# 192 instead of 160 tokens add their experts' V rows by gather; the dense V product runs over 352 token columns

## What is computed

```
q = (x @ w_query)                               # 8 heads, 2 halves of 128
s = einsum('thpc,hpnc->thpn', q, sub_keys)      # scores against 2 x 128 keys
ids, gates = top-16 of the 16 x 16 sums per head, softmax   # 128 experts per token
h = gelu(einsum('td,thkd->thk', x, u_table[ids]))
out = einsum('thk,thkd->td', gates * h, v_table[ids])       # v_table: 16384 x 2048
x = LayerNorm(alpha * x + out)
```

## Time and profile before

| | us |
|---|---|
| median of 3 runs | 3607.54 |
| lowest, highest | 3605.48, 3608.09 |
| profiled execution, its own time | 3631.05 |
| its span, first to last instruction | 3629.3 |

### The profile page before, as it was taken

The page is one execution under the profiler, slowest core; times in us unless marked ns, Lnnn a source line. Parts: engine busy times, 40 slices in busy tenths (PEclk is TensorE's granted clock), DMA queues, the critical chain, the costliest instruction groups (busy, mean ns, idle before and its releaser), DMA issues. The chain is left out here.

```text
span 3629.3 us, 62687 instructions
## 1 busy us (share of the span) xinstructions
PE 3519.3 (97%) x25376; PEld 3466.7 (96%) x25376; DVE 2730.9 (75%) x3476; ACT 1186.3 (33%) x1155; POOL 1843.4 (51%) x1107
## 2 busy tenths in 40 slices
PE   8999999898999999999999999998899999999997
PEld 7999999898999999999999999998899999999996
DVE  4866959624899777777777777774588888888876
ACT  2332332314222234444444444443222222222223
POOL 3443533445444577868787860003366666665321
PEclk9999999899999999999999999999899999999998
DMA  4222212563235578888888887776699899999962
GB/s 152 74 75 78 80 72 79 212 254 128 82 104 177 184 211 220 224 230 219 231 224 226 224 226 229 217 229 246 236 354 357 346 356 360 347 358 351 357 264 96
DMA packets 466252, 788.24 MB, mean 217 GB/s; under 512 B 78976, under 2 KB 376384, under 8 KB 402384
## 3 DMA queue, kind: packets, MB, share of 16 engines
q1 hardware_dynamic: 337920, 547.99, 45.8%
...
## 5 line engine op out<-in xcount | busy, mean ns | idle before, releaser
L616 POOL TENSOR_TENSOR wl<-wraw,wh 128x512 fp32r<-128x512 f32 x352 | 536.3, 1554 | 696.9 <-ACT wh L1114 689.0
L667 POOL DMA_INDIRECT g_scratch<-picks,g_col x384 | 684.1, 1782 | 175.6 <-issue 148.7
L1114 ACT ACTIVATE wh<-wraw 128x2048 fp32r<-128x2048 f32 x216 | 414.0, 1917 | 1008.3 <-PE ps L1030 715.2
L1030 PE MATMUL ps<-Wh,wh 128*128 128x384 f32 x2048 | 688.4, 336 | 13.6 <-issue 6.0
L1030 PE MATMUL ps<-Wl,wh 128*128 128x384 f32 x2048 | 687.4, 336 | 6.3 <-issue 6.3
L1030 PE MATMUL ps<-Wh,wl 128*128 128x384 f32 x2048 | 687.3, 336 | 6.2 <-issue 6.1
L998 PE MATMUL ps<-xh,wl 128*128 128x272 f32 x1792 | 518.5, 289 | 0.0
L998 PE MATMUL ps<-xl,wh 128*128 128x272 f32 x1792 | 515.5, 288 | 0.0
L998 PE MATMUL ps<-xh,wh 128*128 128x272 f32 x1792 | 515.0, 287 | 0.0
L715 PE MATMUL ps<-xh,wh 128*128 128x272 f32 x2304 | 488.8, 294 | 22.2 <-DVE ext L1664 11.9
L715 PE MATMUL ps<-xh,wl 128*128 128x272 f32 x2304 | 479.4, 290 | 0.0
...
## 6 DMA issues: line engine op xcount, KB each, us to landing
wraw<-in_u_t SPq DMA_DIRECT2D x128, 1024.0 KB
...
wraw<-in_v_t SPq DMA_DIRECT2D x128, 1024.0 KB
...
```

Source lines behind the costliest of these rows:

```text
L616: ins = nc.gpsimd.tensor_tensor(wl[:, u, part], wraw[:, u, part], f(wh[:, u, part]), ALU.subtract)
L667: nc.gpsimd.indirect_dma_start(g_elem, bass.IndirectOffsetOnAxis(ap=idx, axis=0), gate, None, compute_op=ALU.add).then_inc(g_put, 16)
L1030: ins = mat(out, w[:, u, d * EG + e], m[:, e], start=(begin and e == 0 and w is wh and m is Wh[v]), stop=(end and e == EG - 1 and w is wl))
L1114: go(wh[:, u], wraw[:, u], ACT.Copy).then_inc(whi, 1)
```

## The change

TD becomes T - P - RT = 352 with RT = 64, and so SD = 192. REST is now 64 tokens, spread over NB = 2 partitions each: XSLOTS = 64, ALL = 192 slots over the same 110 steps. The dense products, `gt`, `hg`, `wt` and the additions have 352 columns. `Wh` and `Wl` keep rows of 384 (and so their places in memory). Of the third tile of 128 dense tokens, gates of only 96 are scattered; the number of scatters stays. `y_x` now gives 16 x 64 columns, twice what the bank TURN has free at once, so `fold` is done in halves: 8 matmuls of 64 columns after PE's tile m = 6 of group 14 and 8 after m = 7, with a DVE addition after each. The REST lists are packed by 6 small DMAs instead of 12.

```diff
-TD = 384
+RT, NB = 64, 2
+TD = T - P - RT
 SD = T - TD
-NGC = TD // GC
+NGC = -(-TD // GC)
-NB = P // TS
-XSLOTS = SLOTS // NB
+XSLOTS = -(-SLOTS // NB)
...
-TOPK_TILES = ((0, P), (P, P), (2 * P, P), (T - P, P), (TD, TS))
+TOPK_TILES = ((0, P), (P, P), (2 * P, P), (T - P, P), (TD, RT))
...
-        Wh = [at(f"Wh{v}", [P, EG, TD], F32R, X0 + v * 2 * EG * ROWD) for v in range(2)]
+        WROW = 384 * 4
+        Wh = [at(f"Wh{v}", [P, EG, 384], F32R, X0 + v * 2 * EG * WROW)[:, :, 0:TD] for v in range(2)]
...
-                    nc.gpsimd.dma_start(dst[to], src[:, fr]).then_inc(pk_s, 16)
+                    nc.gpsimd.dma_start(dst[to, 0:fr.stop - fr.start], src[:, fr]).then_inc(pk_s, 16)
...
-                if m == EG - 2:
-                    pe.wait_ge(y_sp_u, 4)
+                if m >= EG - 2:
+                    half = m - (EG - 2)
+                    pe.wait_ge(y_sp_u, 4 + half)
                     pe.wait_ge(y_sp_s, 2)
-                    for k in range(KT):
-                        ins = mat(ps[:, TURN, k * TS:(k + 1) * TS], y_x[:, k * P:(k + 1) * P], fold[:],
+                    for j in range(HK):
+                        k = half * HK + j
+                        ins = mat(ps[:, TURN, j * RT:(j + 1) * RT], y_x[:, k * P:(k + 1) * P], fold[:],
                                   start=True, stop=True)
                     ins.then_inc(y_turn, 1)
...
+            for x in (x_ids, x_hid, x_gate):
+                C.done(nc.vector.memset(x[:], 0), dve)
+            C.done(tt_(fold[:], ident[:, 0:RT], ident[:, RT:2 * RT], ALU.add), ids_s)
...
+                if n == (NG - 2) * EG + EG - 1:
+                    v_.wait_ge(y_turn, 5)
+                    a_ = acc[:, 0:HK, TD:T - P]
+                    C.inc(stt_(a_, a_, ALPHA, ps[:, TURN, 0:HK * RT].rearrange("p (k t) -> p k t", k=HK),
+                               ALU.mult, ALU.add), y_sp_u)
...
-            v_.wait_ge(y_turn, 5)
+            v_.wait_ge(y_turn, 6)
```

More of the change, by code:

```diff
@@ L265, in program @@
[L265 to L271 removed]
+        XB = XSLOTS * 4
+        x_ids, x_hid = [at(n, [P, XSLOTS], U32, S0 + 15520 + k * XB) for k, n in enumerate(("x_ids", "x_hid"))]
@@ new lines, in program @@
+        x_gate, x_h, x_w = [at(n, [P, XSLOTS], F32, S0 + 15520 + (2 + k) * XB) for k, n in enumerate(("x_gate", "x_h", "x_w"))]
+        fold = at("fold", [P, RT], F32, S0 + 15520 + 5 * XB)
+        o = 15520 + 5 * XB + RT * 4
+        r_ids, r_hid = [at(n, [RT, SLOTS], U32, S0 + o + k * SLOTS * 4) for k, n in enumerate(("r_ids", "r_hid"))]
+        r_f = at("r_f", [RT, SLOTS], F32, S0 + o + 2 * SLOTS * 4)
+        o += 3 * SLOTS * 4
+        assert o + 5 * SLOTS * 4 + 4 <= 21760
+        zeros = at("zeros", [P, 4, TD], F32, S0)
@@ L275, in program @@
-        Wl = [at(f"Wl{v}", [P, EG, TD], F32R, X0 + v * 2 * EG * ROWD + EG * ROWD) for v in range(2)]
-        G0 = X0 + 4 * EG * ROWD
+        WROW = 384 * 4
+        Wh = [at(f"Wh{v}", [P, EG, 384], F32R, X0 + v * 2 * EG * WROW)[:, :, 0:TD] for v in range(2)]
+        Wl = [at(f"Wl{v}", [P, EG, 384], F32R, X0 + (v * 2 + 1) * EG * WROW)[:, :, 0:TD] for v in range(2)]
+        G0 = X0 + 4 * EG * WROW
         gath = [at(f"gath{v}", [P, D], F32, G0 + v * D * 4) for v in range(3)]
@@ L361, in program @@
             sem("slots_done"), sem("slots_turned"), sem("turned_used"))
-        sh_in = [sem(f"slot_h_in{b}") for b in range(ALL // HB)]
+        sh_in = [sem(f"slot_h_in{b}") for b in range(-(-ALL // HB))]
         sv_in = [sem(f"slot_v_in{b}") for b in range(3)]
@@ L1350, in score_evict @@
                 go(sc[:, slot, 0:4].rearrange("p q k -> p (q k)"), ps[:, 4 + 2 * (slot % 2), :], ACT.Copy)
-                go(sc[0:TS, slot, 4], ps[0:TS, 5 + 2 * (slot % 2), 0:P], ACT.Copy).then_inc(s_out, 1)
+                go(sc[0:RT, slot, 4], ps[0:RT, 5 + 2 * (slot % 2), 0:P], ACT.Copy).then_inc(s_out, 1)
             for n in range(SC):
@@ L1870, in _ @@
             C.done(ts_(s_h[:], s_w[:], float(SD), s_tok[:], ALU.mult, ALU.add), dve)
-            C.done(ts_(s_h[:], s_h[:], float(TS), None, ALU.add), dve)
+            C.done(ts_(s_h[:], s_h[:], float(RT), None, ALU.add), dve)
             C.done(cp(s_hid[:], s_h[:]), dve)
             def rest(a):
-                return picks[0:TS, a, REST].rearrange("p h k -> p (h k)")
+                return picks[0:RT, a, REST].rearrange("p h k -> p (h k)")
             C.done(stt_(r_f[:], rest(1), float(P), rest(2), ALU.mult, ALU.add), dve)
             cp(r_ids[:], r_f[:])
-            C.done(ts_(r_f[:], r_f[:], float(SD), s_tok[0:TS], ALU.mult, ALU.add), dve)
+            C.done(ts_(r_f[:], r_f[:], float(SD), s_tok[0:RT], ALU.mult, ALU.add), dve)
             C.done(cp(r_hid[:], r_f[:]), dve)
-            C.done(tt_(fold[:], ident[:, 0:TS], ident[:, TS:2 * TS], ALU.add), dve)
-            for b in range(2, NB):
-                ins = tt_(fold[:], fold[:], ident[:, b * TS:(b + 1) * TS], ALU.add)
-                C.done(ins, ids_s if b == NB - 1 else dve)
+            for x in (x_ids, x_hid, x_gate):
+                C.done(nc.vector.memset(x[:], 0), dve)
+            C.done(tt_(fold[:], ident[:, 0:RT], ident[:, RT:2 * RT], ALU.add), ids_s)
             def flat(a):
@@ L2026, in slot @@
                 if s % HB == 0:
[L2027 removed]
+                    n = min(HB, ALL - s)
+                    v_.wait_ge(sh_in[s // HB], 16 * n)
                     if s < SLOTS:
@@ L2031, in slot @@
                     else:
-                        C.done(tt_(x_w[:], x_h[:], x_gate[:], ALU.mult), dve)
+                        b = slice(s - SLOTS, s - SLOTS + n)
+                        C.done(tt_(x_w[:, b], x_h[:, b], x_gate[:, b], ALU.mult), dve)
                 v_.wait_ge(sv_in[s % 3], 16 * (s // 3 + 1))
@@ L2098, in _ @@
                     slot(s)
-            v_.wait_ge(y_turn, 5)
-            a_ = acc[:, :, TD:T - P]
-            C.done(stt_(a_, a_, ALPHA, ps[:, TURN].rearrange("p (k t) -> p k t", k=KT), ALU.mult, ALU.add), dve)
+            v_.wait_ge(y_turn, 6)
+            a_ = acc[:, HK:KT, TD:T - P]
+            C.done(stt_(a_, a_, ALPHA, ps[:, TURN, 0:HK * RT].rearrange("p (k t) -> p k t", k=HK),
+                        ALU.mult, ALU.add), dve)
             nc.vector.memset(fsum1[:], 0.0)
```

31 lines of the change are left out of this document (11 added, 20 removed).

## The result

| | us |
|---|---|
| before, median of 4 runs (lowest, highest) | 3607.07 (3605.48, 3608.09) |
| after, median of 4 runs (lowest, highest) | 3622.36 (3617.20, 3627.01) |
| after / before, 95% interval | 1.0045 (1.0033 to 1.0057) |
| profiled execution of after, its span | 3617.2, 3615.4 |

The change makes the kernel 15 us slower, where 3602.5 was forecast as the likeliest time. A second measurement, at the end of the study, gave 3622.92 beside 3607.89, ratio 1.0040 (1.0018 to 1.0063).

A forecast was written before the change was run, and what follows sets the result against it. PE bound the kernel, with DVE and the transfers close behind. Groups with slots +1.9, steps without slots -9.6 and the sparse part's end +2.7 gave -5.0 us on the median 3607.54: 3602.5 us, range 3574 to 3640.

The forecast's parts named there:

- the transfers set the pace, 380 GB/s: 3623: Rival for the slot-carrying groups: coupled DMA queues hold only 380 GB/s, 68.2 us a group, 3623 us; chance 0.28 (380 to 365).
- PE's ledger, 7.68 us a step: V stage: 32 fewer columns save PE 0.64 us a step, giving 7.68 us a step, 61.4 a group of eight.
- DVE's ledger, 63.9 us a group: V stage: DVE's work rises from 59.6 to 63.9 us a group, through more slots and slightly shorter narrow operations.
- The DMA ceiling, 403 GB/s: V stage: the DMA engines can carry 403 GB/s, so a group's 25.9 MB take 64.3 us.
- How the three add up: Groups with slots: PE, DVE and DMA together give 66.7 us a group, +0.14, or +1.9 us over 13.75 groups.
- a group is 65.3 us: Groups with slots: PE's pace with DVE's uneven heavy steps, before transfers, gives 65.3 us, 1.3 less than before.
- DVE's two long tiles (8.4 and 10.6 us): V stage: DVE falls 1 us behind at m = 5 and 2.3 at m = 6, stretching two tiles to 8.4 and 10.6 us.
- POOL's ledger: V stage: a V gather and its h gather cost 4.1 us against a slot every 4.7 us, so POOL fits at 88%.
- The sentence in brackets below that ledger: POOL shares its SBUF interface with DVE; if POOL instructions lengthen as DVE fills up, that adds to the slower case.
- The steps without slots, -9.6: The 18 steps without slots, in groups 0, 14 and 15: PE gets its 0.64 us in 15, -9.6 us.
- the end, +2.7: End of the sparse part: fold of twice the columns +1.2 us, longer wait for DVE's last slot +1.5; bounds 0 and +6.
- The signs to look for: V stage: PE waits for `wl`, ACT for `wraw`, DVE for `gath`; if the last two carry the loss, transfers are the cause.

The follow-up runs named there:

- e3: The changed kernel, but each V gather fetches half of each row and DVE adds that half twice: 3603.71 us, ratio 0.9999 to the kernel before.
- e4: The changed kernel with all gathers kept, but DVE adds only half of each gathered row per slot: 3539.57 us, ratio 0.9814 to the kernel before.
- e1: The changed kernel with only 160 of its 192 slots, so narrow columns alone: 3551.08 us, ratio 0.9845 to the kernel before.
- e14: e3 with the preparation of the next group's weights spread over the group's steps: 3579.50 us, ratio 0.9897 to the kernel before.
- e5: The changed kernel with idle matmuls filling PE's waits before tiles m = 7 and m = 0 in groups 2 to 13: 3615.41 us, ratio 1.0031.
- e10: e3 with idle matmuls filling PE's waits before tiles m = 7 and m = 0: 3599.46 us, ratio 0.9967 to the kernel before.

## Why the prediction was wrong

It said 3602.5, with the bounds 3574 and 3640; 3622.4 is on the other side of no change. The time lies next to the rival "the transfers set the pace, 380 GB/s: 3623". That is a coincidence; the mechanism is not that rival's: with half the bytes (e3) groups are still 67.8 us, and with less DVE work the same bytes go at 410 GB/s (e4).

- *PE's ledger, 7.68 us a step*: right; group 15 has 7.74 and 7.73, and e1 gained 54 us.
- *DVE's ledger, 63.9 us a group*: right. The late group of after, 68.4 us, less DVE's 4.3 us of waits is 64.1, and e14 runs at 64.3.
- *The DMA ceiling, 403 GB/s*: right, if low by 2% (410 over 200 us).
  The 358 GB/s that the prediction weighed, of the Trainium skill, "DMA: Bandwidth & Descriptors", Bandwidth, is passed by 15% in e4; the measurement decides. What the page says of single-core runs, nearer to 435, agrees.
- *"How the three add up", a group of 66.7 us, +0.14*: this is the step that failed. Measured 68.9, +1.8 on a group of before, times 13 is 23.4 us in place of 1.9. (The base was low as well: the group of before, taken as 66.56, is 67.1 on average, as four of the 13 have a step of some 9.5 us.) In the prediction's own terms, "a group is 65.3 us" for DVE and PE alone was 67.8 (e3), 2.5 too low, and the transfers' 1.4 on top of it were 1.1. Three things were mis-sized:
  - *"DVE's two long tiles (8.4 and 10.6 us)"*, which are PE's tiles m = 7 and 0 with the wait before them, were 9.62 and 12.12. The lengths of DVE's heavy steps were right: 9.82, 9.65 and 10.46 from split to split for 9.7, 9.7 and 10.6. What failed is how far DVE is behind when they begin. The sum gives m = 3 one slot and so enters them ahead. By `slots_at` this holds for groups 1 to 7 only; from group 8 on the steps with one slot are m = 2 and 6, and m = 3, 4 and 5 all carry two. In e3, where hardly a transfer is late, tile m = 7 takes 8.8 to 9.4 us in groups 1 to 7 and 9.6 from group 8 on, and the eight tiles from there 67.1 and 68.3 us on average. So the shift can account for at most 1.2 us of the later groups; the earlier ones too are 1.8 above 65.3. PE waits 4.5 us for `wl` in the late group, and in the light steps behind DVE cannot make up for it, since it follows PE there: it then waited 4.3 us for PE and ACT where the sum had left it 1.4. e3 against e14 prices the unevenness at 3.6 us a group.
  - *PE's clock after its waits* was not in the sum at all: 1.6 us in a tile m = 0, in 7 groups of after, but most of it is taken back elsewhere, so that 4 to 7 us in all are what e5 and e10 can give it, at the edge of the noise.
  - *POOL's ledger, "4.1 us, POOL fits, at 88%"*: it is 4.73 us, 66.0 a group. The 1.55 us of an h gather came from a mean over the whole page, which holds the 32 issued ahead of all slots, while DVE adds nothing; in the V stage of before it was 1.74 already, and it grew to 2.20. The sentence in brackets below that ledger named the mechanism, and the sum left it out. What this cost is not shown: e3 has nearly the same POOL times and DVE waits 0.5 us a group for gathers, so it can only be a part of the 1.1 us.
- *The steps without slots, -9.6, and the end, +2.7*: the first 16 steps gave -8.5, where some -3 were due, since the first eight steps with slots took 62.3 us; the last eight and the tail gave -1.0, where -3.7 were due (ten tiles at -0.64, +2.7). PE's timeline of after at the fold answers to the earlier trace rows:

```profile
3505.88 3.26 PE L1099 MATMUL ps<-fold,y_x 128*128 128x64 f32 x16 [4.12 <-DVEq L2090]
...
3518.62 1.89 PE L1099 MATMUL ps<-fold,y_x 128*128 128x64 f32 x16
```

  Its length grew by 1.4 us (+1.2 in the sum), PE's wait for the last slots by 3.3 (+1.5 in the sum).
- *"I know of no step that this difference touches"*: the 23.5 us between the profiled execution and the median are most likely the stall in group 0 (27.8 us by the estimate above), which overlaps the stretch of the earlier trace rows. Applying the sum to the median was right, but the earlier trace rows describes the stall, not the usual course of group 0.
- *The signs to look for* served: the waits for `wl` came, those of ACT for V tiles and of DVE for gathers too. "If those two carry the loss, it is the transfers" would have misled: e3 takes nearly all of them away and keeps 67.8 us.
